# Five conditioning rows moved from the end of the down projection's splits to between the evictions of its output tiles

## The reference

```python
x = x + g2 * conv_glu(modulate(rms_norm(x, norm2_w), sh2, sc2), ffn_w_up, ..., ffn_w_down)   # first block's last step
x = rms_norm(x, final_norm_w)                                      # first block's result

c_act = jax.nn.silu(c)                                             # second block
mod = (c_act @ ada_w[i] + ada_b[i])[:, None, :]                    # 1024 x 6144 weights, 24 MB
sh1, sc1, g1, sh2, sc2, g2 = jnp.split(mod, 6, axis=-1)
h = rmsnorm(x, mix_norm_pre[i]) * (1.0 + sc1) + sh1                # input of the second block's QKV product
```

## Time and profile before

| | us |
|---|---|
| median of 3 runs | 1310.9 (1310.49 to 1311.98) |
| the profiled execution | 1311.85 |
| its span | 1310.0 |
| PE busy | 1259.6 (96%) |
| DVE, ACT, POOL busy | 822.5, 681.6, 702.0 |
| mean granted clock of TensorE | 0.984 |

### The profile page before, as it was taken

The page is one execution under the profiler, slowest core; times in us unless marked ns, Lnnn a source line. Parts: engine busy times, 40 slices in busy tenths (PEclk is TensorE's granted clock), DMA queues, the critical chain, the costliest instruction groups (busy, mean ns, idle before and its releaser), DMA issues.

```text
span 1310.0 us, 21756 instructions
## 1 busy us (share of the span) xinstructions
PE 1259.6 (96%) x7760; PEld 1070.7 (82%) x7760; DVE 822.5 (63%) x1452; ACT 681.6 (52%) x1273; POOL 702.0 (54%) x582
## 2 busy tenths in 40 slices
PE   8999999999998999999999999999989999999998
PEld 1688888676787799999887788766869999998886
DVE  2577652668537988888886371686267787773113
ACT  3812545685536356666323464587365655653232
POOL 0335153268343957887766824354608666666561
PEclk9999999999998999999999989899999999999999
DMA  9417549032132743223585412110302223233221
GB/s 392 193 49 276 191 161 178 17 115 80 66 116 110 284 167 118 108 96 120 182 327 204 145 65 80 50 50 34 129 1 97 98 99 125 96 103 122 96 96 65
DMA packets 27412, 166.87 MB, mean 127 GB/s; under 512 B 2976, under 2 KB 5280, under 8 KB 8656
## 3 DMA queue, kind: packets, MB, share of 16 engines
q1 hardware_dynamic: 25328, 151.31, 32.6%
q10 hardware_dynamic: 2016, 14.68, 3.0%
HBM read 163.85 MB, written 6.32 MB: 130 GB/s over the span
## 4 chain that ended last, share of the span: by engine, by line
PE 77%; DVE 8%; POOL 4%; ACT 4%; DMA 3%; issue 3%; SPq 0%; DVEq 0%; ACTq 0%; POOLq 0%
PE bank L1641 26%; PE bank L297 21%; PE bank L357 13%; PE bank L333 5%; POOL w_lo L290 2%; DMA ada_ring<-ada_dram 2%; PE bank L1514 1%; DVE ada_ring L2418 1%; PE bank L1486 1%; PE bank L777 1%; PE bank L586 1%; DVE arena L2482 1%; DMA w_raw<-w_dram 1%; PE bank L600 1%; PE bank L572 1%
## 5 line engine op out<-in xcount | busy, mean ns | idle before, releaser
L290 POOL TENSOR_TENSOR w_lo<-w_raw,w_hi 128x512 fp32r<-128x512 f32 x168 | 258.7, 1571 | 331.4 <-ACT w_hi L281 331.4
L297 PE MATMUL bank<-h_hi,w_hi 128*128 128x512 f32 x512 | 205.5, 401 | 8.7 <-DVE h_lo L473 4.1
L1641 PE MATMUL bank<-arena_rounded,w_hi 128*128 128x256 f32 x1152 | 203.2, 278 | 0.0
L297 PE MATMUL bank<-h_lo,w_hi 128*128 128x512 f32 x512 | 202.0, 395 | 0.0
L297 PE MATMUL bank<-h_hi,w_lo 128*128 128x512 f32 x512 | 201.8, 394 | 0.0
L1357 POOL TENSOR_TENSOR w_lo<-w_raw,w_hi 128x512 fp32r<-128x512 f32 x108 | 141.1, 1308 | 102.4 <-ACT w_hi L1869 100.8
L281 ACT ACTIVATE w_hi<-w_raw 128x2048 fp32r<-128x2048 f32 x46 | 88.1, 1916 | 167.4 <-PE bank L357 60.6
L1641 PEld LDWEIGHTS bank<-arena_rounded,w_hi 128*128 128x128 f32 x1152 | 174.9, 188 | 0.0
L1641 PE MATMUL bank<-arena_rounded,w_lo 128*128 128x256 f32 x576 | 159.3, 277 | 0.0
L1641 PE MATMUL bank<-h_hi,w_hi 128*128 128x256 f32 x432 | 122.2, 283 | 1.4 <-DVE arena L2334 1.1
L297 PEld LDWEIGHTS bank<-h_hi,w_hi 128*128 128x128 f32 x512 | 97.9, 191 | 31.4 <-issue 6.7
(11 more groups left out here) (329 smaller groups left out, 2896.7 us busy)
## 6 DMA issues: line engine op xcount, KB each, us to landing
w_raw<-w_dram SPq DMA_DIRECT2D x92, 1024.0 KB, 4.8
ada_ring<-ada_dram SPq DMA_DIRECT2D x30, 1024.0 KB, 5.2
ada_ring<-ada_dram ACTq DMA_DIRECT2D x14, 1024.0 KB, 4.9
arena<-ada_dram SPq DMA_DIRECT2D x4, 1024.0 KB, 9.9
arena<-x_dram SPq DMA_DIRECT2D x2, 2048.0 KB, 11.7
bias_copies<-bias_rows SPq DMA_DIRECT2D x1, 4096.0 KB, 17.7
arena<-bias_copies SPq DMA_DIRECT2D x4, 768.0 KB, 5.8
ada_ring<-rpb_dram SPq DMA_DIRECT2D x16, 128.0 KB, 9.3
```

What stands on the lines that cost most here:

```text
L290: last = nc.gpsimd.tensor_tensor(w_lo[b % 2][:, part], w_raw[b % 2][:, part], w_hi[b % 2][:, part], ALU.subtract)
L297: last = nc.tensor.matmul(bank[:, :], w[:, ft, k, :], x[:, k, :], start=k == first and m == 0, stop=k == final and m == 2)
L1641: last = nc.tensor.matmul(product_at[p], w[:, k], x[:, k], start=k == 0 and m == 0, stop=k == 3 and m == 2)
```

## The change

The conditioning rows 19 to 23 (five rows, ten half dots) are taken out from behind `hidden_low` 9 and 11 and done one at a time behind the evictions of tiles 0 to 4, ahead of that tile's `add_squares`. The five tiny instructions come behind the eviction of tile 5. Their loads move in SP's order: block 46, row 19, block 47, row 20, block 48, row 21, block 49, rows 22 and 23, block 50. `SQF` gets a buffer of its own (1536 values behind `SQ2`), and ACT's wait for `ada_used` 48 goes. `TURNED_BEHIND` writes an order of POOL's in another way; it is the same order.

```diff
--- before.py
+++ after.py
@@ -478,7 +478,7 @@
         t_sum, t_high, t_low, w_sum, seven_low, seven_snap, seven_sum, seven_more, a21_copied, seven_taps = map(sem, (
             "t_sum", "t_high", "t_low", "w_sum", "seven_low", "seven_snap", "seven_sum", "seven_more", "a21_copied", "seven_taps"))
 
-        SQ1, SQ2, SQF = A(A_TMP, 3, 512), A(A_SQ, 3, 512), view(ada, 0, 3, 512)
+        SQ1, SQ2, SQF = A(A_TMP, 3, 512), A(A_SQ, 3, 512), A(A_SQ + 1536, 3, 512)
         HB1 = A(A_BT, 2, 512)
         XN2, HB2 = A(A_T, 2, 512), A(A_T + 1024, 2, 512)
         tap_buf = [HID[:, 20 + u, :] for u in range(2)]
@@ -491,7 +491,8 @@
             "wdt_ready", "hctx_scaled", "xr_done", "v2_done", "v2_free", "mod2_ready", "wdt_h"))
         F_OUT, F_UP, F_QKV, F_UP2 = 24, 32, 76, 88
         ROWS_UP = 2 * PLAIN1 - 3
-        DOWN_ROWS = ((9, 10), (11, 12), (13, 14), (15, 16), (17, 18), (19, 20), (21, 22, 23))
+        TURNED_BEHIND = {B_UP + 2: 2, B_UP + 4: 0, B_UP + 5: 3}
+        DOWN_ROWS, LATE_ROWS = ((9, 10), (11, 12), (13, 14), (15, 16), (17, 18)), range(19, 24)
 
         t_parts = [[view(over, 16384 - A_OVER + 4096 * part + 1024 * t, 4, 256) for part in range(2)] for t in range(4)]
         h_parts = {(k, n): [h[:, 4 * k:4 * k + 4, 256 * n:256 * n + 256] for h in (h_hi, h_lo)] for k in range(2) for n in range(2)}
@@ -1306,9 +1307,12 @@
             load_block(sp, B_DOWN + 2)
             load_block(sp, B_DOWN + 3)
             for b in range(B_DOWN + 4, B_QKV + 1):
-                if b < B_DOWN + 10:
+                if b < B_DOWN + 8:
                     load_rows(*DOWN_ROWS[b - B_DOWN - 3])
                 load_block(sp, b)
+                if b >= B_DOWN + 8 and LATE_ROWS[0] + b - B_DOWN - 8 < 24:
+                    load_rows(LATE_ROWS[0] + b - B_DOWN - 8)
+            load_rows(*LATE_ROWS[4:])
             load_block(sp, 50)
             sp.wait_ge(mod2_ready, 1)
             sp.wait_ge(g_split, 11)
@@ -1435,8 +1439,8 @@
             low_aside(pool, B_UP + 1)
             for b in range(B_UP + 2, up1.first):
                 low(pool, b)
-                if b < B_UP + 5:
-                    low_turned(up1, (2, 0, 3)[b - B_UP - 2])
+                if b in TURNED_BEHIND:
+                    low_turned(up1, TURNED_BEHIND[b])
             pool_sevens(up1)
             lows(B_DOWN + 2, 6)
 
@@ -2159,8 +2163,6 @@
             def both_squares(f):
                 act.wait_ge(down_free, f + 1)
                 squares(act, 3, f, XR[:, f, :], SQ2, scale=final_eps[:, f:f + 1])
-                if f == 0:
-                    act.wait_ge(ada_used, 48)
                 if f >= 2:
                     act.wait_ge(sqf_used, f - 1)
                 nc.scalar.activation(SQF[:, f % 2, :], XR[:, f, :], ACT.Square).then_inc(sqf_done, 1)
@@ -2653,21 +2655,25 @@
             for t in range(4):
                 hidden_low(5 + t, slice(4 + 2 * t, 6 + 2 * t), 2 * (t % 2))
                 rows_behind(1 + t)
+            def conditioning():
+                dve.wait_ge(ada_used, 48)
+                link(nc.vector.scalar_tensor_tensor(out=gain3, in0=mod2[:, 8:16], scalar=1.0, in1=par_("mixpre"), op0=ALU.add, op1=ALU.mult))
+                nc.vector.tensor_tensor(gain3, gain3, par_("final"), ALU.mult)
+                nc.vector.scalar_tensor_tensor(out=gain4, in0=mod2[:, 32:40], scalar=1.0, in1=par_("ffnpre"), op0=ALU.add, op1=ALU.mult)
+                nc.vector.tensor_tensor(post1, mod2[:, 16:24], par_("mixpost"), ALU.mult)
+                nc.vector.tensor_tensor(post2, mod2[:, 40:48], par_("ffnpost"), ALU.mult).then_inc(mod2_ready, 1)
+
             hidden_low(9, slice(12, 14), 0)
-            rows_behind(5)
             hidden_low(10, slice(16, 18), 2)
             hidden_low(11, slice(14, 16), 0)
-            rows_behind(6)
-            dve.wait_ge(ada_used, 48)
-            link(nc.vector.scalar_tensor_tensor(out=gain3, in0=mod2[:, 8:16], scalar=1.0, in1=par_("mixpre"), op0=ALU.add, op1=ALU.mult))
-            nc.vector.tensor_tensor(gain3, gain3, par_("final"), ALU.mult)
-            nc.vector.scalar_tensor_tensor(out=gain4, in0=mod2[:, 32:40], scalar=1.0, in1=par_("ffnpre"), op0=ALU.add, op1=ALU.mult)
-            nc.vector.tensor_tensor(post1, mod2[:, 16:24], par_("mixpost"), ALU.mult)
-            nc.vector.tensor_tensor(post2, mod2[:, 40:48], par_("ffnpost"), ALU.mult).then_inc(mod2_ready, 1)
             for f in range(DC):
                 dve.wait_ge(half_used, used_after(B_DOWN + 6) + f + 1)
                 nc.vector.scalar_tensor_tensor(out=XR[:, f, :], in0=ps[f][:, :], scalar=modb[:, 24 + f:25 + f], in1=XR[:, f, :],
                                                op0=ALU.mult, op1=ALU.add).then_inc(down_free, 1)
+                if f < len(LATE_ROWS):
+                    add_ada2(LATE_ROWS[f])
+                if f == len(LATE_ROWS):
+                    conditioning()
                 if f < DC - 1:
                     add_squares(dve, 3, f, SQ2)
 
```

## The result

The changed kernel is slower. In 16 runs of each, its median is 1315.8 us (1310.1 to 1320.5) and that of the kernel before 1311.8 us (1310.5 to 1314.4); the ratio is 1.003, with a 95% interval of 1.002 to 1.004, so +4.0 us. It lies outside the stated range of 1308.8 to 1314.3, and above the bound of 1315.0 too.

The account below looks back on a forecast made before the run. TensorE was taken to bound the kernel, at 77% of the span. −1.90 for the pause, +0.8 and +1.3 for new waits gave +0.2; handovers added 0.4: 1310.9 + 0.6 = 1311.5 us, range 1308.8 to 1314.3.

Parts of the forecast that it names:

- the bound of 1315.0: Upper limit of the time, +4.1 us: VectorE's rows at the full 4.5 us and row 22's load landing late.
- The pause of 1.90 us: TensorE's idle time before block 46, released late by GpSimd; the change was to remove it, −1.90 us.
- two new waits of TensorE: TensorE would wait 0.8 us for block 48's low part before tile 6 and 1.3 us at `mean_head`.
- The replay of VectorE's path: VectorE's evictions, late rows and sums of tiles 0 to 6, timed one by one, ending at 747.8.
- conditioning 743.6: After tile 5's eviction at 743.1, VectorE's five tiny instructions were to be done by 743.6.
- B: VectorE falls behind for good before `mean_head`, 6.5 us a tile against TensorE's 5.46; +2.6 us, 1313.5; chance 0.18.
- the 747.8 of the replay: Time at which VectorE's sum of tile 6 was to be ready, making TensorE wait 1.3 us at `mean_head`.
- one sum of squares 1.28: Price in us of each VectorE sum of squares behind a tile, from 1.11 to 1.51 in the rows.
- The wait before tile 6: TensorE would wait 0.8 us after tiles 2 to 5, until GpSimd finished block 48's low part at 736.9.
- 5.7 us behind: VectorE's lag behind TensorE at tile 2: ready at 719.9, evicted at 725.6.
- Rival C: A new pause at 736 or 746 brings a half-clock stretch onto tiles 6 and 7; +1.9 us, 1313.4; chance 0.06.

## Why the prediction was wrong

**Right.** The pause of 1.90 us and its cause: half dots beside block 46. POOL's block 46 at 5.03 (said 5.24), block 47 at 7.48 (7.5), block 48 at 7.89 (8.06); ScalarE's copy of 48 behind the eviction of tile 2; two new waits of TensorE at just these places; no price for the buffer; the loads with slack, but for 0.30 us at row 22. The replay of VectorE's path up to tile 5 was off by up to 0.9 us on the way and by 0.1 at its end: VectorE came to the conditioning at 743.24 on the clock of the kernel before (1.31 later than in its own trace, from the two starts of block 45), where I had 743.1.

**The step that failed is "conditioning 743.6"**, half a microsecond for the five tiny instructions. They took 3.11 us, 2.6 more. I took the rows of before, where the five ran while GpSimd had no piece in hand, and did not ask of the tiny instructions what I had asked of the large ones. From there on VectorE had no slack, as the prediction says under B: each microsecond is one of the time. So the sum of tile 6 was ready at 750.28 on that clock, 2.5 later than the 747.8 of the replay, and TensorE waited 2.82 us instead of 1.3. Taking the five out of the path gave 2.2 us back on the chip.

Other terms were off too, and cancelled, which is luck.
- "one sum of squares 1.28". Measured 1.69 each for the five behind half dots and conditioning (1.77 with its overlap): +0.4 each. The rows of before had 1.11 to 1.51 since the sum there waited for ScalarE and often met a piece half done; behind another instruction that had just let GpSimd in, it waits for a whole one. The last sum, of tile 6, met no piece at all and took 0.7: −0.6.
- Rows 20 and 22 took 3.8 us and not 4.5 (22 with its wait for the load), since only one of two half dots met a piece in full: −1.4 for both. Row 23 took 3.8 and not 3.5.

**The wait before tile 6** was 1.50 us instead of 0.8, and not because VectorE was later than I had it: it evicted tile 2 a little earlier, and ScalarE's copy of block 48 ended at 728.3 on the clock of before, where I had 728.8. The term that was too small is GpSimd's sums of tiles 0 to 2, ahead of block 48: priced at 4.1 us, from rows without half dots beside them, and 5.8 here, so that the low part began at 729.75 and not at 728.8. This did not set the end, and no run here tests it by itself. (In the same replay, "5.7 us behind" counts the eviction itself; the eviction of tile 2 began 5.0 us late. Nothing was worked out from it.)

**Wrong: the clock at nothing.** Rival C had it at 0.06 and at 1.9 us. It came on top of the longer wait, not instead of it: `mean_head` and the rest of tile 7 ran at 0.75, `mean_last` at 0.50, together +1.1 us. From `mean_head` to the end of tile 7 the three profiles with the wait of 2.8 us have 0.75, 0.72 and, without loads, 0.76; all others, with waits of 1.1 us or less there, have 1.00. My reason against it, that the pause at block 46 left the clock at 1.00, rested on one execution; the buffer-alone run shows the same pause with half clock behind it.

**Rival B** had the place and the side of what came, and I gave it 0.18. Its way there was another: rows 21 and 23 at 4.5 us. They took 3.4 and 3.8, and what B had not priced, the conditioning, made up for them.

**The range.** From 1310.9 as the starting point; 16 runs put the kernel before at 1311.8, 0.9 higher. The bound of 1315.0 had been worked out, and the range was drawn inside it; the measured 1315.8 is above both.

## What to carry to other kernels

Where VectorE and GpSimd share time, count VectorE's instructions with two SBUF operands (and its copies within SBUF), not their elements: each one, down to 128x8, may cost a whole GpSimd piece more. GpSimd's own small sums pay in the same way, and what stands behind them is late by it. Before moving work behind a tile, add up that engine's queue per tile against TensorE's per tile, with every such instruction at its price beside GpSimd; three rows fitted under these evictions and gave 3.4 us, five did not and lost 4.0. Small instructions that nobody waits for yet should go where the other engine is idle, not where the source code has room.

## What the runs showed of the hardware that I had not expected

- An instruction of 128x8 on VectorE, 0.15 to 0.17 us alone, took 1.20 to 1.27 us where it met a whole GpSimd instruction of 128x512, and 0.51 to 0.85 where it met part of one. Where GpSimd was at work, one or two of the five in a row met a whole one, and the next of them took 0.15. 64-wide half dots took 1.31 instead of 0.28.
- Moving one of the two operands of a half dot to PSUM took the mutual slowing away on both engines (0.74 us a piece of 512, block 47 at 5.25).
- A copy of 128x512 within SBUF on VectorE, with one input, took 0.42 us alone and 1.28 beside a GpSimd piece.
- A pause of 1.76 us of TensorE was followed by 3.4 us at half clock in one execution, and one of 1.74 was not in another. Around a pause, one execution is no proof of the clock.
